# State-space stage of a two-block decoder kernel: where turned tokens are multiplied by the step size

## The reference

```
xbc = jax.nn.silu(causal_dwconv(xbc_raw, conv_w, conv_b)).astype(jnp.float32)
xs = xbc[..., :SSD_WIDTH].reshape(b, t, SSD_HEADS, SSD_HEADDIM)
...
dt = jax.nn.softplus(dt_raw.astype(jnp.float32) + dt_bias.astype(jnp.float32))
...
xdt = x * dt[..., None]
...
cb = jnp.einsum('bclgn,bcsgn->bcgls', cm, bm)
y_diag = jnp.einsum('bcgrls,bcsgrp->bclgrp', cb[:, :, :, None] * lm, xdt)
...
y = y + d_skip.astype(jnp.float32)[:, None] * xs
yg = (y.reshape(b, t, SSD_WIDTH) * jax.nn.silu(z.astype(jnp.float32))).reshape(b, t, SSD_GROUPS, -1)
```

## Time and profile before

| | |
|---|---|
| median of 3 runs | 3504.55 us (3503.25 to 3504.89) |
| the profiled execution's own time | 3508.61 us |
| its span | 3506.8 us |
| PE busy | 3466.6 us (99%) |
| PE weight loads busy | 2910.8 us (83%) |
| DVE busy | 1484.2 us (42%) |
| ACT busy | 579.3 us (17%) |
| mean granted clock of PE | 0.994 of full speed |

### The profile page before, as it was taken

One profiled execution on the slowest core, in us unless ns is written; L12 is line 12 of the kernel. 1 busy time (PEld: TensorE's weight loads), 2 busy tenths in 40 slices (PEclk: granted clock), 3 DMA queues, 4 the chain that ended last, 5 costly groups with the idle time before them and its releaser, 6 DMA issues.

```text
span 3506.8 us, 47599 instructions
## 1 busy us (share of the span) xinstructions
PE 3466.6 (99%) x19963; PEld 2910.8 (83%) x19963; DVE 1484.2 (42%) x2653; ACT 579.3 (17%) x1466; POOL 44.6 (1%) x82
## 2 busy tenths in 40 slices
PE   9999999999999999999999999999999999999999
PEld 8888888888888998888878877877778888888788
DVE  1426631335367452513335626424333356363343
ACT  1012200011011101011000115311120001252111
POOL 1000000000000000000000000000000000000000
PEclk9999999999999999999999999999999999999999
DMA  6443343543543203644425443333344364433432
GB/s 209 144 145 120 107 153 125 150 139 102 156 140 124 73 3 121 219 139 144 144 77 188 143 124 121 97 120 108 134 143 154 91 191 144 130 123 97 144 121 72
DMA packets 436015, 454.29 MB, mean 130 GB/s; under 512 B 25211, under 2 KB 412720, under 8 KB 435280
## 3 DMA queue, kind: packets, MB, share of 16 engines
q1 hardware_dynamic: 433408, 444.68, 40.1%
q0 software_dynamic: 2096, 5.19, 0.4%
q10 hardware_dynamic: 320, 1.70, 0.1%
HBM read 449.45 MB, written 2.10 MB: 129 GB/s over the span
## 4 chain that ended last, share of the span: by engine, by line
PE 97%; DVE 1%; ACT 1%; DVEq 0%; issue 0%; POOL 0%; DMA 0%; ACTq 0%; POOLq 0%
PE bank L1824 32%; PE bank L279 18%; PE bank L376 10%; PE bank L1935 9%; PE bank L410 5%; PE bank L308 3%; PE bank L1999 3%; PE bank L1493 3%; PE bank L1053 3%; PE bank L292 2%; PE bank L1908 1%; PE bank L1986 1%; PE bank L1958 1%; PE bank L1861 0%; PE bank L439 0%; PE bank L578 0%
## 5 line engine op out<-in xcount | busy, mean ns | idle before, releaser
L1824 PE MATMUL bank<-xnT,ring 128*128 128x272 f32 (+2 forms) x4992 | 1133.8, 389 | 0.0
L1824 PEld LDWEIGHTS bank<-xnT,ring 128*128 128x128 f32 (+1 forms) x4992 | 941.2, 189 | 178.3 <-issue 0.7
L279 PE MATMUL bank<-xnT,ring 128*128 128x272 f32 (+1 forms) x2816 | 633.2, 388 | 1.6 <-ACT wk L803 1.0
L279 PEld LDWEIGHTS bank<-xnT,ring 128*128 128x128 f32 x2816 | 534.7, 190 | 99.7 <-issue 3.3
L376 PE MATMUL bank<-xnT,ring 128*128 128x256 f32 x1536 | 342.6, 382 | 0.7 <-ACT wk L1227 0.7
L376 PEld LDWEIGHTS bank<-xnT,ring 128*128 128x128 f32 x1536 | 289.7, 190 | 40.9 <-ACT wk L1227 1.1
L1935 PE MATMUL bank<-G,ring 128*128 128x272 f32 (+1 forms) x1024 | 243.4, 391 | 0.0
L1935 PEld LDWEIGHTS bank<-G,ring 128*128 128x128 f32 x1024 | 192.7, 191 | 36.3 <-issue 3.6
L410 PE MATMUL bank<-G,ring 128*128 128x256 f32 x768 | 166.3, 379 | 0.0
L410 PEld LDWEIGHTS bank<-G,ring 128*128 128x128 f32 x768 | 145.8, 190 | 19.9
L459 DVE RECIPROCAL G<-G 128x272 f32<-128x272 f32 (+3 forms) x25 | 149.4, 5977 | 1.8
(11 more groups left out here) (537 smaller groups left out, 2924.1 us busy)
## 6 DMA issues: line engine op xcount, KB each, us to landing
ring<-in_w_in SPq DMA_DIRECT2D x156, 2048.0 KB, 8.3
ring<-in_w_out SPq DMA_DIRECT2D x32, 2048.0 KB, 8.7
ring<-in_w_br SPq DMA_DIRECT2D x12, 2048.0 KB, 8.4
ring<-in_w_out SPq DMA_DIRECT2D x16, 1024.0 KB, 11.3
G<-in_x POOLq DMA_DIRECT2D x2, 1024.0 KB, 9.2
wk<-in_pool_w POOLq DMA_DIRECT2D x2, 1024.0 KB, 9.4
ring<-in_w_in SPq DMA_DIRECT2D x4, 512.0 KB, 5.5
out<-G SPq DMA_DIRECT2D x8, 256.0 KB, 2.2
```

Of the source, the lines that this page charges most:

```text
L279: mm = pe.matmul(bank[j][:, first:T], ring[:, s, k, j * P:(j + 1) * P], rhs[:, k, first:T], start=(k == 0), stop=(k == KT - 1))
L1824: mm = pe.matmul(out_, ring[:, s, k, c:c + m], xnT[:, k, first:T], start=(k == 0), stop=(k == KT - 1))
```

## The change

ACT no longer copies the turned tokens. Its six copies per half and the `done()` behind them are left out; the line `turns["act"].go(6)` only keeps its count of turns right. DVE no longer waits for `b2_act` at the head of a half. It waits for each turn itself, reads the 512 columns from the turn bank, multiplies them by the step sizes and writes the product into `tok3`, in six instructions instead of three, each of which raises `turn_free`. PE's list and its waits are the same; what raises the semaphore is another engine. The table `tok_turns` is filled while PE's list is written and tells DVE the numbers of the turns.

```
--- before.py
+++ after.py
@@ layers_pe
                 for half in range(2):
+                    tok_turns.append(turns["pe"].n)
                     for i, (t0, n) in enumerate(TT):
@@ layers_act
                 for half in range(2):
-                    for i, (t0, n) in enumerate(TT):
-                        for q in range(2):
-                            b = turned()
-                            act.activation(tok3[0:n, i, 512 * q:512 * q + 512], b[0:n, :], ACT.Copy).then_inc(turn_free, 1)
-                    done()
+                    turns["act"].go(6)
                     for pair in range(8):
@@ layers_dve
                 spread_steps(0)
                 for half in range(2):
-                    wait("b2_act")
+                    u = tok_turns[2 * layer + half]
                     for i, (t0, n) in enumerate(TT):
-                        xt = tok3[0:n, i, :].rearrange("p (h d) -> p h d", d=64)
-                        v.tensor_tensor(xt, xt, cols2[0:n, i, 16 * half:16 * half + 16].unsqueeze(2).to_broadcast([n, 16, 64]),
-                                        ALU.mult)
+                        for q in range(2):
+                            u += 1
+                            v.wait_ge(turn_full, u)
+                            h0 = 16 * half + 8 * q
+                            v.tensor_tensor(tok3[0:n, i, 512 * q:512 * q + 512].rearrange("p (h d) -> p h d", d=64),
+                                            tbank(u)[0:n, :].rearrange("p (h d) -> p h d", d=64),
+                                            cols2[0:n, i, h0:h0 + 8].unsqueeze(2).to_broadcast([n, 8, 64]),
+                                            ALU.mult).then_inc(turn_free, 1)
                     to("b2_pe")
```

More of the change, by code:

```diff
@@ L1680, in build @@
         out_banks = []
+        tok_turns = []
         def begin(layer):
```

## The result

| | before | after |
|---|---|---|
| median of the runs on one chip | 3503.59 us (8 runs, 3498.17 to 3504.89) | 3513.36 us (8 runs, 3510.34 to 3516.45) |
| profiled execution, own time | 3508.6 us | 3516.45 us |
| its span | 3506.8 us | 3514.7 us |
| DVE busy | 1484.2 us | 1486.5 us |
| ACT busy | 579.3 us | 565.7 us |

The ratio is 1.0031, with a 95% interval from 1.0022 to 1.0040: the change costs 9.8 us. It takes 13.6 us of work off ACT and adds 2.3 us to DVE. Neither bounds the kernel, so neither figure explains the time. In the changed file the lines of PE's part of this stage have numbers higher by one or two: the turns are L1888, the products of `cb` L1893, of the pairs L1910, the wait ahead of half 0 L1871, the turned probabilities L1976.

What follows compares the result with a forecast made beforehand. PE, busy 99% of the span, was taken to bound the kernel. Stalls of 7.7 us plus 5.0 us for the clock, 12.7 us, on a median of 3504.55 gave 3517.3 us, range 3511 to 3522.5.

Steps and rivals of the forecast that it cites:

- Late starts and reads, 7.7 us: At the turns (L1886), DVE starts reading later than ACT, 6.5 us, and reads take longer, 1.2 us.
- One bound of the reads: Upper bound at the turns: 0.69 us per read without overlap, 0.2 us per half more, 2.0 us in all.
- The price of a read from the bank: DVE's reads at the turns: a skill page's dearer bank access would add 0.8 us; left out because the rows disagree.
- The clock, 5.0 us: PE's clock falls behind half 1's new stall of 3.4 us in both layers, 2.5 us each.
- rival A: The clock also falls in half 0: two more falls of 2.5 us, 3522.3 us; chance 0.17.
- Rival B: The clock does not fall at all; only the stalls at the turns remain, 3512.3 us; chance 0.18.
- Rival C: Not slower: PE's lateness is given back at the first attention head (L1974), 3504.8 us; chance 0.07.
- Rival D: ACT's copies were the limit at the turns and six direct reads are quicker, 3501.2 us; chance 0.03.
- No wait at `b2_pe`: The half's first products are ready by 2171.2 or earlier, PE asks at 2175.3, so no new wait.
- earlier decays worth nothing: ACT's next decays come 3.8 us earlier, but PE wants the multiplied one 1.6 us after it is ready: no gain.

Runs made afterwards that it cites:

- change_again: The changed kernel, unaltered, run once more on another chip: 3517.81 us beside 3502.58 for the kernel before, ratio 1.0040.
- change_third: The changed kernel, unaltered, with a third trace: 3517.44 us beside 3505.11 for the kernel before, ratio 1.0038.
- pe_filler2: The changed kernel with unneeded matmuls in PE's stalls at the turns and in the wait at L1871: 3511.76 us beside 3505.11 before, ratio 1.0021.
- h0_dve: The changed kernel with DVE's direct reads in half 0 only, ACT copying in half 1: 3507.44 us beside 3503.57 before, ratio 1.0012.
- pe_filler: The changed kernel with unneeded matmuls behind the second turn, 3 in half 0 and 6 in half 1: 3516.86 us, ratio 1.0035 to before.
- h1_dve: The changed kernel with DVE's direct reads in half 1 only, ACT copying in half 0: 3514.67 us, ratio 1.0031 to before.
- early_reads: The changed kernel with DVE's reads moved ahead of `rope` (half 1) and two ahead of the spreads (half 0): 3510.07 us beside 3502.58 before, ratio 1.0014.
- six_banks: The changed kernel with reads moved early and each half's last four turns put in free work banks: 3503.47 us beside 3502.58 before, ratio 0.9999.

## Why the prediction was right, and where it was off

The sign, the mechanism and the range held: 3513.4 us against 3517.3 forecast, in a range from 3511 to 3522.5; +9.8 us against +12.7 in the first comparison, +15.2 and +12.3 in `change_again` and `change_third`.

- **Late starts and reads, 7.7 us.** Measured by `pe_filler2`: 7.8. The stalls came as written (3.4 and 3.3 us in half 1; 1.54 for 1.5 in half 0 of layer 0), the first read starts right behind `rope` (a gap of 0.07 us), a read with its release takes 2168.06 - 2167.31 = 0.75 us for 0.74 expected. The waits at L1888 sum to 8.9 us and not "about 11". In half 0 of layer 1 the stall was only 0.56 us, since the clock was down already (in `change_third`, where it was still up, 1.42 us and 9.6 in all), and the smaller ones of the later turns show up as waits of the weight load (0.33 us ahead of PEld), not of PE. One bound of the reads was added up wrongly: 0.69 against 0.67 us for six reads is 0.1 us per half and not 0.2; the value does not use it.
- **The price of a read from the bank.** The page "Perfetto Trace Analysis" of the Trainium skill, section "Optimizing Scalar/DVE Operations", would have it dearer than one from SBUF. The new line gives 0.689 us beside 0.693 from SBUF, so the trace does not agree.
- **The clock, 5.0 us.** The size of the term was near (4.5 us in the first trace, 6.0 in the other two), its make-up was wrong. The step that failed is that the clock falls in half 1 alone, "there in both layers", at 2.5 us a fall: it fell at all four places, in each of three traces of the change, and against `pe_filler2` nine of the twelve falls cost 0.8 to 1.5 us, the other three 1.9 to 2.2. That is rival A's place at a lower price than A's. My reasoning was that 1.5 us is shorter than 2.31; the runs show a fall behind it all the same (in `h0_dve`, whose only new stalls are those of half 0, the fall begins during them in both layers). I had also taken the 1.8 us of L1871 for harmless by itself, and it is not always: with both waits filled (`pe_filler2`) there was no fall in half 0, with the second alone filled (`pe_filler`) one of two remained, and it began right behind L1871. The page "TensorE: Matmul & The Clock Gate" of the Trainium skill, section "HAM oscillation — how this bites in real kernels", says that waits between bursts of matmuls let the clock fall and that the next burst starts cold. The traces agree: in half 0 of layer 1 the turns behind the wait of 1.81 us took 1.97 us instead of 1.09.
- **Rival B** (stalls alone, 3512.3) has the nearest number to the measured median, but for the wrong reason: the places lost 12.35 us, not 7.8. The sum of places and the measured time differ because the clock falls elsewhere by turns. Before, it had fallen at both first heads (19.2 and 16.4 us), after at neither (14.3 and 13.1), which is 8.1 us between these two traces. The rest of these two traces can be placed as well: 1.8 us more ahead of the first turn of layer 0, 1.3 more between the first head of layer 0 and the turns of layer 1, 0.5 more between the pairs and the heads. 12.3 - 8.1 + 3.6 = 7.8 us is the difference of the two executions (3516.45 and 3508.61). Whether the faster heads are an effect of the change or of the execution stays open: `change_again` was slow at the first of them (16.0). The difference between +9.8 and +15.2 us for one and the same kernel is not explained either.
- **Rival C** fell: PE still waits at L1976, 2.6 us, for DVE. **Rival D** fell: no place got shorter.
- **No wait at `b2_pe`, earlier decays worth nothing:** both hold. The second decay is multiplied by 2175.48, PE asks for it at 2180.5, 5 us later, and L1910 has no wait.

## What to carry to other kernels

When a step is given to another engine, look up when that engine would come to it in its own list, beside the time at which it is ready: the difference goes into the producer's stall, and here it could be read off the trace of before to a tenth of a microsecond. The work taken off ACT bought nothing here, no place got shorter by it; the same fused reads cost nothing in half 1 once they stood ahead of work that nobody was waiting for. Where banks are free at that point, use them: with early reads and six banks PE did not wait at the turns at all, and with the clearing out of the way as well that version gained 10.3 us. Six banks with late reads were not run, so it is not shown that they make the order of the reads indifferent.

## What I had not expected of the hardware

- The granted clock fell during a stall of 1.54 us that follows one of 1.82 us and a few short matmuls. Behind 1.8 us alone it fell in some traces (`h1_dve`, `early_reads`) and not in others (`before`, `six_banks`).
- What a fall costs goes first by how long the clock stays down. The 4.9 us at the first head belong to 10.2 us at the lower clock; where it was down for 3.4 us at a first head the loss was 1.7 us (16.0 against 14.3). In the four places 3.4 to 6.8 us cost 0.8 to 2.2 us.
- Falls are not a property of the kernel alone. At the first heads the same stall was followed by a loss of 4.9 us in one trace and of nothing in others, and traces of one unchanged program differ there (14.3 and 16.0 us). With effects of 10 us in 3500 a single trace cannot price a change; lengths of places can, and medians beside a reference on the same chip to a few us (the change measured +9.8, +12.3 and +15.2).
- Matmuls whose result is thrown away, put into both waits, kept the clock up in all four places, with a median 5.7 us lower. Put into the new stalls alone (`pe_filler`) they kept it up in three and lowered no time.
